# One stage in place of four before a sparse attention, and the roots of a normalisation kept

## The reference

```python
def rmsnorm(x, gain): return x * lax.rsqrt(mean(x * x) + eps) * gain        # over the 1024 channels
def gated_deltanet(qkv, a, b, z, conv_w, ...):
    qkv = silu(causal_depthwise_conv(qkv, conv_w))                          # width 4, 768 channels
    beta = sigmoid(b); g = -exp(a_log) * softplus(a + dt_bias)
    ...                                                                     # chunked recurrence
def rwkv7_time_mix(rw, z, mu, ...):
    rw = rw + mu * (shift_prev(rw) - rw)                                    # 7 x 128 channels
    w_log = -softplus(-(w0 + tanh(wd) @ w_up)) - 0.5; a = sigmoid(a0 + ad @ a_up)
    ...
def spatial_gating(u, v, z, ...):
    v = layernorm(v, ln_gain, ln_bias)                                      # over groups of 64 channels
    return u * (einsum(tril(w_s), v) + b_s) * silu(z)
def sparse_attention(q, k, v, ...):
    kc = compress_blocks(k, pos, w1, w2)    # gelu(blocks of 32 positions + pos, @ w1) @ w2, stride 16; vc too
    ...                                     # attention over compressed, selected and windowed keys
```

## Time and profile before

| | us |
|---|---|
| median of the runs shown (3) | 3028.54 |
| lowest and highest | 3027.52, 3029.04 |
| the profiled execution's own time | 3029.41 |
| its span | 3027.5 |
| PE busy in the span | 2655.7 (88%) |
| DVE busy | 1578.1 (52%) |
| ACT busy | 1056.1 (35%) |
| POOL busy | 30.0 (1%) |

### The profile page before, as it was taken

One profiled execution on the slowest core, in us unless ns is written; L12 is line 12 of the kernel. 1 busy time (PEld: TensorE's weight loads), 2 busy tenths in 40 slices (PEclk: granted clock), 3 DMA queues, 4 the chain that ended last, 5 costly groups with the idle time before them and its releaser, 6 DMA issues. The chain is left out here.

```text
span 3027.5 us, 38198 instructions
## 1 busy us (share of the span) xinstructions
PE 2655.7 (88%) x15105; PEld 2107.3 (70%) x15105; DVE 1578.1 (52%) x3003; ACT 1056.1 (35%) x2163; POOL 30.0 (1%) x70
## 2 busy tenths in 40 slices
PE   6977368699975998989998999979989999989999
PEld 4865257588754765777776888857657777768887
DVE  4314776676635548534336666445585343354444
ACT  3124332333225536444223222245454432232221
POOL 0000200000000000000000000000000000000000
PEclk8997689799987999999999999989999999999999
DMA  4210000366620120121324555212101213313230
GB/s 140 74 44 1 17 6 3 88 198 194 197 84 28 67 73 1 42 75 43 99 84 153 181 183 179 84 56 84 56 1 42 76 46 96 107 60 112 84 111 28
DMA packets 212219, 249.57 MB, mean 82 GB/s; under 512 B 13295, under 2 KB 125898, under 8 KB 212042
## 3 DMA queue, kind: packets, MB, share of 16 engines
q1 hardware_dynamic: 177056, 193.30, 19.7%
q10 hardware_dynamic: 34986, 53.84, 5.4%
HBM read 243.70 MB, written 2.10 MB: 81 GB/s over the span
## 5 line engine op out<-in xcount | busy, mean ns | idle before, releaser
L2048 ACT ACTIVATE weights_hi<-weight_ring 128x512 fp32r<-128x512 f32 (+1 forms) x240 | 143.9, 602 | 435.2 <-PE bank L2089 409.3
L2065 DVE TENSOR_TENSOR weights_lo<-weight_ring,weights_hi 128x512 fp32r<-128x512 f32 (+1 forms) x240 | 156.0, 653 | 236.2 <-ACT weights_hi L2048 236.2
L2815 ACT ACTIVATE weights_hi<-weight_ring 128x1024 fp32r<-128x1024 f32 x128 | 135.3, 1057 | 265.5 <-PE bank L2895 264.7
L2089 PE MATMUL bank<-h_hi,weights_hi 128*128 128x512 f32 x512 | 210.7, 411 | 16.9 <-DVE h_lo L2065 10.4
L2895 PE MATMUL bank<-h_hi,weights_hi 128*128 128x512 f32 x512 | 203.7, 398 | 19.4 <-DVE h_lo L341 19.4
L2374 PE MATMUL bank<-chunk_hi,h_hi 128*128 128x512 f32 x448 | 184.3, 411 | 30.4 <-DVE h_lo L341 26.0
L2089 PE MATMUL bank<-h_lo,weights_hi 128*128 128x512 f32 x512 | 205.0, 400 | 0.0
L2895 PE MATMUL bank<-h_lo,weights_hi 128*128 128x512 f32 x512 | 203.6, 398 | 0.0
L2089 PE MATMUL bank<-h_hi,weights_lo 128*128 128x512 f32 x512 | 202.8, 396 | 0.0
L2895 PE MATMUL bank<-h_hi,weights_lo 128*128 128x512 f32 x512 | 201.2, 393 | 0.0
L2895 PE MATMUL bank<-hidden_hi,weights_hi 128*128 128x512 f32 x512 | 200.0, 391 | 0.0
(11 more groups left out here) (474 smaller groups left out, 5372.9 us busy)
## 6 DMA issues: line engine op xcount, KB each, us to landing
arena<-in_ada_w ACTq DMA_DIRECT2D x48, 1024.0 KB, 5.1
weight_ring<-in_w_in SPq DMA_DIRECT2D x21, 2048.0 KB, 7.6
weight_ring<-in_w_in SPq DMA_DIRECT2D x65, 512.0 KB, 5.2
weight_ring<-in_w_mlp_up SPq DMA_DIRECT2D x16, 2048.0 KB, 8.7
weight_ring<-in_w_mlp_down SPq DMA_DIRECT2D x16, 2048.0 KB, 8.0
weight_ring<-in_w_out SPq DMA_DIRECT2D x6, 2048.0 KB, 7.9
weight_ring<-in_w_in SPq DMA_DIRECT2D x10, 1024.0 KB, 7.0
weight_ring<-in_w_branch_a SPq DMA_DIRECT2D x16, 512.0 KB, 6.4
```

The costliest lines, as they stand in the source:

```text
L2048: act.activation(hi, src, ACT.Copy).then_inc(*hi_done.one())
L2065: dve.tensor_tensor(lo, src, hi.bitcast(F32), ALU.subtract).then_inc(*lo_done.one())
L2089: ins = pe.matmul(out, ws[a_][:, n % PIECES, k - k0, :], tile["x"][b_][:, k, :], start=k + a_ + b_ == 0, stop=last[n] and k == k1 - 1 and ...
L2815: act.activation(ws[0][:, t % 2], src[t // 4][:, :, c % 4 * P:c % 4 * P + P], ACT.Copy)\
```

## The change

- `nsa_compress`, `nsa_tables`, `spatial_gating` and the rest of `mixer_preparation` become one stage, `preparations`, ahead of the sparse attention. Nine of its transfers are started by SP, the six of the compression by ACT as before.
- The six convolutions and seven shifts move into the tile loop of `p1`, on DVE one per output tile (tiles 7 to 12 and 13 to 19), with the silu on ACT a tile later. POOL's masks run in the sparse attention's block (`beside`).
- `y_nsa` is turned at the end of `operands`: eight transposes on PE and one copy 128x1024 on ACT.
- `rms` squares into eight buffers; DVE adds them up and one matmul by ones takes the place of eight. With `ahead=True` (`rms1` and both `rms_mix`) the four weight pieces that the next stage began with are split in the normalisation.
- At the starts of `p1`, the queries and keys and the MLP, DVE takes scaling and second parts by turns, the second part two rows behind.
- The roots of `rms1` stay in the arena at `ROOTS_AT`, and `rms1_again` is gone. The buffers of the recurrences leave the ring, whose feed on SP runs beside them; `operands` has 15 arena units for 16, and two of its values share one.

```diff
+    def vector_row(self, dve, k):
...
+        dve.scalar_tensor_tensor(to(self.dst[:, k, :]), from_(self.xT[:, k, :]), self.gain(k), from_(self.rs),
+                                 ALU.mult, ALU.mult).then_inc(*self.scaled.one())
...
+    def vector_and_second(self, dve, second):
+        for k in range(ND + 2):
+            if k < ND:
+                self.vector_row(dve, k)
+            if k >= 2:
+                second(k - 2)
...
-                        act.wait_ge(*self.mm_done.at(k - 1))
-                    act.activation(sq[:, k % 2, :], self.xT[:, k, :], ACT.Square).then_inc(*self.act_ready.one())
+                    act.activation(sq[:, k, :], self.xT[:, k, :], ACT.Square).then_inc(*self.act_ready.step(("square", k)))
+                for _ in range(pieces):
+                    self.w.split_hi(act)
                 seq = self.order(act, self.act_order)
-                act.wait_ge(*self.dve_ready.at(1))
...
                 seq(act.activation(rs, rs, ACT.Ln))
-                act.activation(rs, rs, ACT.Exp, scale=-0.5).then_inc(*self.act_ready.one())
+                act.activation(rs, rs, ACT.Exp, scale=-0.5).then_inc(*self.act_ready.step("root"))
...
-                for k in range(ND):
-                    pe.wait_ge(*self.act_ready.at(k + 1))
-                    pe.matmul(self.bank[0][:], self.ones[:], sq[:, k % 2, :], start=k == 0,
-                              stop=k == ND - 1).then_inc(*self.mm_done.one())
+                pe.wait_ge(*self.dve_ready.after("total"))
+                pe.matmul(self.bank[0][:], self.ones[:], total, start=True, stop=True).then_inc(*self.mm_done.one())
...
-                dve.wait_ge(*self.mm_done.at(ND))
...
+                dve.wait_ge(*self.act_ready.after(("square", 1)))
+                ins = dve.tensor_tensor(total, sq[:, 0, :], sq[:, 1, :], ALU.add)
+                for k in range(2, ND):
+                    seq(ins)
+                    dve.wait_ge(*self.act_ready.after(("square", k)))
+                    ins = dve.tensor_tensor(total, total, sq[:, k, :], ALU.add)
+                ins.then_inc(*self.dve_ready.step("total"))
...
+                dve.wait_ge(*self.mm_done.at(1))
...
+                   .then_inc(*self.dve_ready.step("mean"))
+                for _ in range(pieces - pieces // 2):
+                    self.w.split_lo(dve)
...
+                    if t - 2 in convolved:
+                        c = convolved[t - 2]
+                        act.wait_ge(*self.mixed_dve.after(("conv", c)))
+                        act.activation(qkvT[:, c, 3:], acc[:, c % 2, :], ACT.Silu)\
+                           .then_inc(*self.mixed_act.step(("silu", c)))
...
-                norm.vector(dve)
-                while self.w.next_lo < self.w.pieces_until(("p1", "qkv"), 0):
-                    self.w.split_lo(dve)
...
+                norm.vector_and_second(dve, second)
+                seq = self.order(dve, self.dve_order)
+                def convolve(c):
+                    dve.wait_ge(*self.pool_order.at(1))
+                    dve.wait_ge(*self.evac_dve.at(c + 1))
+                    if c >= 2:
+                        dve.wait_ge(*self.mixed_act.after(("silu", c - 2)))
+                    w = lambda j: self.par[:, PAR["gdn_conv"] + 6 * j + c:PAR["gdn_conv"] + 6 * j + c + 1]
+                    seq(dve.tensor_scalar(acc[:, c % 2, :], qkvT[:, c, 0:T], w(0), None, ALU.mult))
+                    for j in range(1, 4):
+                        ins = dve.scalar_tensor_tensor(acc[:, c % 2, :], qkvT[:, c, j:j + T], w(j), acc[:, c % 2, :],
+                                                       ALU.mult, ALU.add)
+                        if j < 3:
+                            seq(ins)
+                    ins.then_inc(*self.mixed_dve.step(("conv", c)))
...
+                    seq(dve.tensor_tensor(acc[:, c % 2, :], rwT[:, c, 0:T], rwT[:, c, 1:], ALU.subtract))
+                    dve.scalar_tensor_tensor(rwT[:, c, 1:], acc[:, c % 2, :], mu, rwT[:, c, 1:], ALU.mult, ALU.add)\
...
+                    if t - 1 in convolved:
+                        convolve(convolved[t - 1])
+                    if t - 1 in shifted:
+                        shift(shifted[t - 1])
...
+            if beside is not None:
+                block.gpsimd(beside)
...
+    def preparations(self):
...
+        self.y_nsa = self.ysT[:, 0:2, :].rearrange("p k t -> p (k t)").rearrange("p (i c) -> p i c", i=NT)
...
+                act.wait_ge(*mixers.all_of_stage(96))
...
+                act.wait_ge(*dve_done.after("var"))
+                seq(act.activation(rstd, rstd, ACT.Ln))
+                act.activation(rstd, rstd, ACT.Exp, scale=-0.5).then_inc(*act_done.step("root"))
                 for j in range(2):
-                    act.wait_ge(*self.mm_done.at(j + 2))
+                    act.wait_ge(*mm.after(f"hidden{j}"))
                     act.activation(hidden[0:E, j, :], self.bank[1 + j][0:E, 0:NC], ACT.Gelu_apprx_tanh)\
-                       .then_inc(*self.act_ready.one())
...
+                    act.wait_ge(*dve_done.after(("wa", j)))
...
+                    act.activation(two, two, ACT.Sigmoid).then_inc(*act_done.step(("wa", j)))
...
+                for c in range(2):
+                    act.wait_ge(*mm.after(("y", c)))
+                    act.activation(self.ysT[:, 2 + c, :], self.bank[(3, 6)[c]], ACT.Copy).then_inc(*act_done.step(("y", c)))
...
+                pool.wait_ge(*gating.all_of_stage(48))
...
+                pe.wait_ge(*pool_done.after("w_rows"))
...
+                pe.wait_ge(*compress.all_of_stage(16 * 6))
...
+                pe.wait_ge(*act_done.after("tanh"))
+                pe.wait_ge(*mixers.all_of_stage(96))
+                gates(0)
+                pe.wait_ge(*dve_done.after(("blocks", 3)))
+                for p in range(32):
+                    for j in range(2):
+                        ins = pe.matmul(self.bank[1 + j][0:E, 0:NC], w1[half(j), p, :], blocks[half(j), p, :],
...
+                pe.wait_ge(*dve_done.after(("wa", 0)))
+                gates(1)
+                pe.wait_ge(*dve_done.after("wT"))
+                pe.wait_ge(*dve_done.after("normed"))
+                for g in range(H):
+                    ins = pe.matmul(self.bank[4 + g // 2][:, g % 2 * MIX:(g % 2 + 1) * MIX], wT[:, g, :],
...
+                pe.wait_ge(*act_done.after("hidden1"))
...
+                pe.wait_ge(*dve_done.after("y"))
...
+                gates(1)
+                dve.wait_ge(*mm.after("wT"))
...
+                dve.wait_ge(*act_done.after("root"))
...
+                sp.dma_start(w_rows, a["sg_w_s"][0].rearrange("g t s -> t g s")).then_inc(*gating.dma())
...
+                sp.dma_start(up[E:P, :], a["rw_a_up"][0]).then_inc(*mixers.dma())
...
+        self.end_stage("preparations")
...
+                pe.wait_ge(*act_done.after(("F", "A")))
...
+                        ins = pe.transpose(self.bank[4 + c][:, i * P:(i + 1) * P], self.y_nsa[:, i, c * P:(c + 1) * P],
...
+                act.wait_ge(*pe_done.after("nsa"))
+                act.activation(self.ysT[:, 6:8, :].rearrange("p c t -> p (c t)"), two(4), ACT.Copy)\
+                   .then_inc(*act_done.step("nsa"))
...
+        units = self.free_slices
...
+            @block.sync
+            def _(sp):
+                self.w.feed(sp)
...
-                if norm is not None:
-                    norm.vector(dve)
...
+                    norm.vector_and_second(dve, second)
...
+        self.rms(f"rms_mix{l}", gain(0), mod(0), ahead=True)
...
-                self.norm.vector(dve)
                 split(0)
...
+                self.norm.vector_and_second(dve, second)
...
+        self.rms("rms1", col("norm_gain"), ahead=True, rs=self.arena[:, ROOTS_AT:ROOTS_AT + T])
         self.first_projection()
+        self.preparations()
         self.sparse_attention()
-        self.spatial_gating()
-        self.mixer_preparation()
         self.operands()
+        self.w.limit = None
         self.recurrences()
-        self.w.limit = None
-        self.rms("rms1_again", col("norm_gain"))
```

648 lines of the change are left out of this document (301 added, 347 removed).

## The result

| | us |
|---|---|
| changed kernel, median of 4 executions | 2943.01 (2940.19 to 2948.84) |
| kernel before, beside it | 3028.06 (3027.52 to 3029.04) |
| ratio, 95% interval | 0.9721 (0.9704 to 0.9738) |
| profiled execution of the changed kernel | 2940.19, span 2938.0 |
| all 12 executions of the changed kernel, those of two later runs included | mean 2943.4, 2935.7 to 2948.8 |

The forecast was 2940, from 2929 to 2957. The profiled execution came out at 2940.19, where the sum had 2940.6; the median lies 3 us higher. Twelve executions of the changed kernel spread over 13 us, and 25 of the kernel before over 9 (3025.0 to 3034.0). What follows first compares stages, then explains both differences.

A forecast was written before the change was run, and what follows sets the result against it. PE, busy for 88% of the span, was taken to bound the long projections, so gains lay in uncovered stages and starts. The terms summed to -88.8 us: 3029.4 to 2940.6 profiled, 2940 given as median, range 2929 to 2957.

The forecast's parts named there:

- Preparations: Four old stages of 90.5 us become one of 42.6 with a barrier, gain 47.9; bounds for the stage 38 and 47.
- Since the queues are two and mostly empty I take 1.0, nearer to the free end: Start of preparations: 15 transfers starting together delay the blocks by 1.0 us, to 15.7, between 0 and 3.4.
- The prediction's own sign of a wrong sum: Transfers landing later than 12 us into preparations would make the stage's first 15.7 us slip one for one.
- rms1_again: The repeated normalisation goes, -14.8 us; the merge's weights, asked for beside the recurrences, make nothing late.
- Normalisations: One matmul by ones for eight: final and both MLP ones -5.3 us together, 12.0 each; three with weight pieces -0.2 each.
- Starts: First copies come sooner with pieces gone and scaling and second parts alternating: first projection -6.3 us, queries and keys -13.4 together.
- MLPs: At each MLP start only PE's arrears behind DVE's list can go: -1.1 us each, -2.2 together, bounds 0 and -5.6.
- Convolution, masks: Convolution and shift in the first projection cost 0, bounds 0 and 2 us; masks beside the attention cost 0.7 us.
- Operands +1.0: Turning y_nsa at the end of the operands adds one more ACT copy 128x1024 there: +1.0 us.
- attention +0.7: POOL's masks beside the sparse attention catch few of 34 small DVE operations, at 0.42 us each: +0.7, bounds 0 and 14.
- recurrences 0: The recurrences run the same operations with buffers in other places: 0 us, bounds +-1.
- The rival "clock": PE's full speed comes later at each of five starts, up to 2.7 us each: +13, total 2953 us; chance 0.13.

The follow-up runs named there:

- e: Changed kernel with VectorE scaling all eight rows first, then the eight second parts, at the starts of first projection, queries and keys and MLPs: 2955.9 us.
- f: Changed kernel with the four weight pieces split again at the starts of the first projection and the queries and keys, not in the normalisations: 2960.2 us.
- l_after_third: The changed kernel unaltered, run once more beside three others on one chip: 2943.9 us, ratio to the kernel before 0.9715.
- c_warm_preparations: Changed kernel with five 128x512 float32 matmuls whose results nobody reads, put where TensorE waits in preparations: 2941.0 us.
- b: Changed kernel with the compression's six transfers started first in preparations, three per queue, and the gating weights' transposes behind the compression's matmuls: 2944.4 us.
- j_filler_after_attention: Changed kernel with two 128x512 float32 matmuls with unread results after TensorE's last work of the sparse attention: 2943.4 us.
- i: Changed kernel with compression's transfers first and unread matmuls added: five in preparations, two after the attention, twelve in the operands; 2939.3 us, ratio to before 0.9703.
- d: Changed kernel with GpSimd's masks run in preparations, ahead of the tables' selects, instead of beside the sparse attention: 2940.8 us.

## Why the prediction was right, and where not

The mechanisms held in the main, but that the profiled execution met the sum to 0.4 us is luck. Against the sum, preparations came out at +3.0 us in that profile, the recurrences at +2.0, the MLP of layer 0 at +1.1; the attention at -2.7, the operands at -1.5, queries and keys together at -1.1, the three normalisations with weight pieces at -0.9, the merge's first part at -0.8. These cancel. The mean of the twelve executions, 2943.4, is 3.6 us above the 2939.8 that the prediction had for the median.

1. **Preparations: right in kind, 2.2 us short** (42.6 foreseen, 44.8 in the mean). The step that was mis-sized is "Since the queues are two and mostly empty I take 1.0, nearer to the free end". The positions' copy came 3.3 us later than before in the first profile, which is the other end of the bound, 3.4 (2.4 to 3.7 in the nine). The prediction's own sign of a wrong sum, transfers that land later than 12 us into preparations, came true: TensorE's wait for them ended at 13.6 us, and the blocks ended 18.1 us after the start instead of 15.7. That the bound was met so closely doesn't show that its reason was right, since ScalarE's issues grew by 4.7 us. The rest of VectorE's list was met: 30.8 us (31.6 in two of the nine) from that copy to the end against 30.9. Its wait for the second gates was 2.25 us, 1.9 foreseen.
2. **rms1_again: right**, -14.8, and the merge didn't start later; it was even 0.8 to 1.4 us shorter.
3. **Normalisations: right.** 12.0 and 12.95, where the text had 12.0 and 13.0. The sum took 0.2 us for each of the three with weight pieces; they came out 0.4 to 0.6 shorter. They are now the same in every profile, where the same work took 13.3 and 14.8 us before (rms_mlp, mean granted clock 0.87 and 0.77). That fits one matmul in place of eight that run at whatever clock there is.
4. **Starts: right.** First copy 11.5 us into the projection (11.5 foreseen), 11.9 into the queries and keys (882.41 less 870.54; 12.1 foreseen). The reason was only half right, as e and f show: the two edits aren't additive, and the length of one engine's list doesn't say when the others are fed.
5. **MLPs: one of two.** The first copy comes 1.4 us earlier in layer 0, as foreseen within 0.3, yet the stage kept its 374.7 us. ScalarE issues the load of the next layer's modulation behind its first parts, and these now come at VectorE's pace. Before, and after:

```profile
1610.22 0.95 ACTq L362 DMA_DIRECT2D arena<-in_ada_w  x2
```

```profile
1535.60 0.95 ACTq L375 DMA_DIRECT2D arena<-in_ada_w  x2
...
1538.67 0.60 ACT L2876 ACTIVATE arena<-bank 128x512 f32<-128x512 f32 x1 [1.01 <-PE bank L2938]
...
1551.12 0.60 ACT L2876 ACTIVATE arena<-bank 128x512 f32<-128x512 f32 x1 [4.74 <-PE bank L2938]
```

```profile
1541.01 0.49 DVE L388 TENSOR_SCALAR arena<-arena,cond 128x512 f32<-128x512 f32 x1 [2.10 <-DMA arena<-in_ada_w]
```

   The issue is 11.0 us after the stage's start (1524.64) instead of 5.4, VectorE waits 2.10 us for it with the next pieces behind it in its list, and the third copy comes at 26.5 us, as before. The MLP of layer 1 has no such load and kept 0.6 to 1.0 us. I had looked only at what is queued on VectorE. In e_no_turns ScalarE isn't paced, the issue comes 7.7 us after the start, and VectorE's operation follows its weight piece without a wait:

```profile
1544.61 1.22 DVE L2885 TENSOR_TENSOR weights_lo<-weight_ring,weights_hi 128x1024 fp32r<-128x1024 f32 x1
1545.74 0.48 DVE L387 TENSOR_SCALAR arena<-arena,cond 128x512 f32<-128x512 f32 x1
```

   There the copies stand 5.55 us apart from the first on (6.2 and 6.3 now), so that of the 2.6 us by which its first copy is later only 1.2 are left at the third. This bears the reading out; by turns with the issue moved ahead wasn't tried.
6. **Convolution, masks: right**, 0.01 us and at most 0.6. The argument for the masks was wrong in one step: it took GpSimd's 20.74 busy us as a sign against exclusion and as the load that would stand beside the attention. That time did contain waiting (650 ns for a select of 295), and the load is 12.54 us.
7. **Operands +1.0, attention +0.7, recurrences 0: within what the clock moves.** It moves the first by 4.9 us between executions of the same program. For the operands like can be compared with like: at the clock of the kernel before, 0.92 in the first 20 us with the low stretch at their very start, they take 45.42 us (l_after_third) and 45.41 (c_warm_preparations) against 44.28, +1.1 where +1.0 was foreseen. The attention (1.9 us between executions) goes with its mean clock at both ends, 68.23 us at 0.90 (c), 70.34 at 0.85 (first profile), 73.14 at 0.79 (b), and is anywhere from 71.0 to 72.4 at 0.81 to 0.84; its +0.7 can't be read, nor can the recurrences' 0 (1.7 us between executions). The rival "clock" was looked for at the five starts, where it doesn't occur (first projection and queries and keys repeat to 0.2 us), and not in the stages with waits on all sides, where it does. The profiled execution had the best operands, which accounts for 1.7 to 4.9 us against the other two; the stages behind the merge's first part carry another 3.8 us of the third profile's excess (2179.9 us against 2176.0, granted clock 0.94 against 0.95).

## What to carry to other kernels

When transfers that were spread over several stages are brought to one start, don't price them near nothing: here they cost the chain 2.4 to 3.7 us, about the full DMA time of the ones that joined (3.4), and the issues got longer too. Put the ones that the chain needs first ahead of the others. When an engine's list is interleaved, look at everything that the partner engine issues behind its paced part, its transfers too. When two engines may lock one another out, compare the mean time of the same operation with and without the other engine beside it, on both engines. And before an effect of a few us is read from a total, profile the unaltered kernel two or three times: the stages that differ by themselves tell which differences can't be read.

## What the runs showed of the hardware

TensorE's granted clock fell from 1.00 to 0.50 at 327 us in j_filler_after_attention, after 2.00 us busy of 2.00 at 1.00, and while the engine stayed busy (4.00 of 4.00 us at 0.57 in the mean); at 0.50 it stayed for 6 us busy without a gap (in i and in c). With the same instructions it kept 1.00 in another profile. Filling the waits ahead didn't prevent the fall.

An issue on ScalarE's DMA queue, of the weights `w2`, took 2.24 and 1.72 us with six transfers started together and 3.76 and 4.09 with fifteen.

GpSimd's select of 128x64 lasted 1.3 us beside a VectorE operation of 1.23 us (2.60 for two, in d), and its select of 128x128 650 ns in the mean beside the convolutions and shifts against 295 beside the attention, while VectorE's own operations grew little (0.9 us in 24.46).
